# Sample attention: cache pages loaded as 8 KB pieces over every fourth partition, a chunk's loads issued together

## The reference

```python
k_past = cache_k[l][page_table].reshape(bs, past_len, A_HEADS, A_HEAD_DIM)
v_past = cache_v[l][page_table].reshape(bs, past_len, A_HEADS, A_HEAD_DIM)
...
s = jnp.einsum('bqhd,bkhd->bhqk', qi, k, preferred_element_type=jnp.float32) * scale
s = s + fi.transpose(0, 2, 1)[..., :, None] - fk_t[..., None, :]
s = jnp.where(mask, s, -jnp.inf)
p = jax.nn.softmax(s, axis=-1)
return jnp.einsum('bhqk,bkhd->bqhd', p.astype(v.dtype), v)
```

## Time and profile before

| | |
|---|---|
| median of three runs | 3746.3 us (3746.05 to 3747.52) |
| span of the profiled execution | 3747.3 us |
| busy: TensorE, VectorE, ScalarE, GpSimd | 96%, 50%, 48%, 38% of the span |
| sample attention, first value load to last product | about 2,359 to 3,207 us |
| moved by DMA in the span | 590.40 MB, mean 158 GB/s |
| moved in 2,400 to 3,100 us | 232.67 MB, mean 332 GB/s |

### The profile page before, as it was taken

The page is one execution under the profiler, slowest core; times in us unless marked ns, Lnnn a source line. Parts: engine busy times, 40 slices in busy tenths (PEclk is TensorE's granted clock), DMA queues, the critical chain, the costliest instruction groups (busy, mean ns, idle before and its releaser), DMA issues. The chain is left out here.

```text
span 3747.3 us, 54477 instructions
## 1 busy us (share of the span) xinstructions
PE 3585.3 (96%) x17931; PEld 2823.4 (75%) x17931; DVE 1867.7 (50%) x3105; ACT 1810.5 (48%) x3712; POOL 1423.5 (38%) x1072
## 2 busy tenths in 40 slices
PE   8999999999999999999799999899999999799999
PEld 7788888788878888888566666677777777588787
DVE  3134423332123543322557665588888888544432
ACT  4224423445323443543566767677777777311222
POOL 0011122220011122310477777577777777322200
PEclk9999999999999999999799999999999999899999
DMA  4234334324233334333201211699999999544422
GB/s 164 77 120 132 115 128 145 122 96 139 97 108 115 127 132 155 118 126 88 61 18 40 60 38 63 225 329 335 340 335 334 319 338 326 208 155 162 150 90 76
DMA packets 378555, 590.40 MB, mean 158 GB/s; under 512 B 93381, under 2 KB 114485, under 8 KB 378298
## 3 DMA queue, kind: packets, MB, share of 16 engines
q1 hardware_dynamic: 366146, 579.94, 45.9%
q10 hardware_dynamic: 11584, 5.13, 0.5%
q0 software_dynamic: 576, 2.10, 0.2%
HBM read 475.25 MB, written 111.83 MB: 157 GB/s over the span
## 5 line engine op out<-in xcount | busy, mean ns | idle before, releaser
L996 PE MATMUL prj_z_ps<-prj_w_hi,prj_h_hi 128*128 128x512 f32 x2312 | 923.9, 400 | 2.8 <-DVE prj_w_lo L792 2.7
L998 PE MATMUL prj_z_ps<-prj_w_hi,prj_h_lo 128*128 128x512 f32 x2312 | 902.6, 390 | 0.0
L997 PE MATMUL prj_z_ps<-prj_w_lo,prj_h_hi 128*128 128x512 f32 x2312 | 901.2, 390 | 0.0
L1912 POOL TENSOR_TENSOR sa_v_lo<-sa_v_raw,sa_v_hi 128x1024 fp32r<-128x1024 f32 x256 | 609.1, 2402 | 219.7 <-DVE sa_v_hi L2051 219.2
L998 PEld LDWEIGHTS prj_z_ps<-prj_w_hi,prj_h_lo 128*128 128x128 f32 x2312 | 434.3, 188 | 93.7
L996 PEld LDWEIGHTS prj_z_ps<-prj_w_hi,prj_h_hi 128*128 128x128 f32 x2312 | 435.2, 188 | 90.0 <-DVE prj_w_lo L792 5.7
L997 PEld LDWEIGHTS prj_z_ps<-prj_w_lo,prj_h_hi 128*128 128x128 f32 x2312 | 435.3, 188 | 84.8
L1408 POOL TENSOR_TENSOR pa_p_lo<-pa_probs,pa_p_hi 128x512 fp32r<-128x512 f32 (+1 forms) x320 | 367.6, 1164 | 160.9 <-ACT pa_p_hi L1421 143.5
L2045 DVE TENSOR_TENSOR sa_kT_lo<-sa_t_ps,sa_kT_hi 128x512 fp32r<-128x512 f32 x512 | 345.5, 686 | 141.9 <-ACT sa_kT_hi L1934 138.7
L424 POOL TENSOR_TENSOR prj_dist<-prj_cum 128x256 f32<-128x256 f32 x132 | 88.6, 671 | 793.5 <-DVE prj_cum L863 793.5
L1934 ACT CAST sa_kT_hi<-sa_t_ps 128x512 fp32r<-128x512 f32 x512 | 291.1, 590 | 128.6 <-PE sa_t_ps L2198 120.0
(11 more groups left out here) (330 smaller groups left out, 6417.7 us busy)
## 6 DMA issues: line engine op xcount, KB each, us to landing
arena_k_raw<-in_cache_k_dram SPq DMA_DIRECT2D x512, 256.0 KB, 4.1
sa_v_raw<-in_cache_v_dram SPq DMA_DIRECT2D x512, 256.0 KB, 4.3
arena_w_raw<-in_w_main_dram SPq DMA_DIRECT2D x272, 256.0 KB, 4.2
z_scratch<-prj_z_sb SPq DMA_DIRECT2D x272, 256.0 KB
arena_mg<-z_scratch SPq DMA_DIRECT2D x51, 512.0 KB, 4.4
arena_cu<-extp_scratch SPq DMA_DIRECT2D x48, 256.0 KB
arena_x_in<-in_x_all_dram SPq DMA_DIRECT2D x17, 512.0 KB, 3.7
prj_aux<-z_scratch SPq DMA_DIRECT2D x34, 256.0 KB, 2.8
```

The lines of the kernel that those rows point to most:

```text
L996: pe.matmul(out, h_hi[:, slot_of(t), k], hi, start=(k == 0), stop=False)
L997: pe.matmul(out, h_hi[:, slot_of(t), k], lo, start=False, stop=False)
L998: mm = pe.matmul(out, h_lo[:, slot_of(t), k], hi, start=False, stop=(k == KC - 1))
L1912: pool.tensor_tensor(v_lo[:, w % 2, at], v_raw[:, w % RING, at], v_hi[:, w % 2, at].bitcast(F32), ALU.subtract).then_inc(vlo_ready, 1)
```

## The change

A page is still 256 KB and still one DMA. Before, token p of page j went to partition p, 2 KB long, at place j of the slot. Now the page is cut in 32 pieces of four tokens, 8 KB each, and piece r of page j goes to partition 4r + j, filling the whole slot there. Over the four pages of a chunk every partition is filled. At place i of partition 4r + j stands now token 4r + i of page j. Keys and values are laid out alike, so scores and weights agree. The decay rows must follow: ScalarE's `place` reads them in the order place, piece, page instead of straight through.

The waits before the loads are gathered. All four key pages now wait for the four turns of chunk g-3, and all four value pages for both halves of the value chunk three before.

```diff
@@ begin_sample
-                        src = k_view[bass.ds(pages[j], 1)].rearrange("a k x -> (a k) x")
-                        sp.dma_start(arena.k_raw[:, g, j], src).then_inc(arena.k_loaded[g], 16)
+                        src = k_view[bass.ds(pages[j], 1)].rearrange("a (r i) x -> (a r) i x", i=CHUNK_PAGES)
+                        sp.dma_start(arena.k_raw[j::CHUNK_PAGES, g], src).then_inc(arena.k_loaded[g], 16)
@@ attend_sample, sync
             def page(at, j, dst, view, sem):
-                sp.dma_start(dst[:, j], view[bass.ds(at, 1)].rearrange("a k x -> (a k) x")).then_inc(sem, 16)
+                sp.dma_start(dst[j::CP], view[bass.ds(at, 1)].rearrange("a (r i) x -> (a r) i x", i=CP)).then_inc(sem, 16)
 
             def load_k(g, slot, pages):
+                sp.wait_ge(turned, (g - RING + 1) * CP)
                 for j in range(CP):
-                    sp.wait_ge(turned, (g - RING) * CP + (j + 1))
                     page(pages[j], j, k_raw[:, slot], k_view, k_loaded[slot])
 
             def load_v(w, slot, pages, first=False):
+                if not first:
+                    sp.wait_ge(vlo_ready, (w - RING + 1) * 2)
                 for j in range(CP):
-                    if not first and j % (CP // 2) == 0:
-                        sp.wait_ge(vlo_ready, (w - RING) * 2 + (1 if j == 0 else 2))
                     page(pages[j], j, v_raw[:, slot], v_view, v_loaded[slot])
@@ attend_sample, scalar
             def place(g):
                 act.wait_ge(d_loaded[g % 2], 16 * (g // 2 + 1))
                 wait_from(act, added, g - 1)
-                act.copy(addend[0:2 * HEADS, g % 2], d_raw[:, g % 2]).then_inc(d_placed, 1)
+                by_row = d_raw[:, g % 2].rearrange("h (j r i) -> h i r j", j=CP, i=CP)
+                act.copy(addend[0:2 * HEADS, g % 2].rearrange("h (i r j) -> h i r j", i=CP, j=CP), by_row).then_inc(d_placed, 1)
```

## The result

The changed kernel is slower: 3792.89 us median of four runs (3787.2 to 3797.68), against 3746.91 (3746.05 to 3747.78). The ratio on record is 1.0117, 95% interval 1.0104 to 1.0130 (the two medians alone give 1.0123). 3733 us was forecast. The profiled execution took 3787.2 us, with a span of 3785.5, 38.2 us longer than before's.

A forecast was written before the change was run, and what follows sets the result against it. A chain of GpSimd freeing value slots, SyncE's value then key loads, and TensorE was taken to stall chunks. Key waits -14 us, ScalarE +1, made -13 from the 3746.3 median: 3733 us, range 3722 to 3739.

The forecast's parts named there:

- Link 1: SyncE before the value loads: all four value pages wait for GpSimd's second half, fourth key issue 0.76 us later.
- the turn shown: Worked example from the earlier trace: GpSimd done at 2642.84, keys landed by 2651.9, TensorE resumes at 2651.94.
- the far end: Slow end of the forecast: key landing stays at 5.0 us, 0.25 us per chunk lost, +32 us.
- Link 3: Key loads in 8 KB pieces: 405 GB/s instead of 332, last page landing in 3.65 us, keys 0.6 us earlier.
- the break-even of 4.24: Landing time of the last key page, 5.0 - 0.76 us, above which Link 1 outweighs the faster landing.
- The gain: TensorE's key waits, 18.7 us in 109 chunks, 21.4 over the stage; two thirds won, -14 us.
- ScalarE's copy: Strided placing copy: 0 to 0.62 us over 615 ns, covered by the next copy's idle time; 1 us counted.
- link 2: SyncE before the key loads: the batched wait for four turns of chunk g-3 costs nothing, they being long past.
- the start of the stage: First key bursts pause there, values start up to 1.6 us later but are wanted three chunks on: nothing.
- B: Rival: waiting for the whole value slot on SyncE decides, 0 to 0.25 us per chunk, +21, 3767 us; chance 0.18.
- Rival C: Loads get slower, long pieces overlapping worse: 300 GB/s, 7.1 us per chunk, +85, 3831 us; chance 0.05.
- the coarser rule: Only transfers spanning all 128 partitions reach all 16 ports; for 32 partitions half of 332 GB/s, 12.8 us per chunk.

The follow-up runs named there:

- e1_waits: Kernel before with only the key and value waits gathered, 2 KB pieces and plain placing copy kept: 3770.91 us, ratio 1.0057.
- e8_4kb: Pages in 64 pieces of 4 KB over every second partition, values going out by halves, keys waiting pair by pair, placing copy in two: 3782.71 us, ratio 1.0091.
- e3_order_new: Changed kernel with SyncE's order altered, values of chunk g-3 instead of g-2 behind the keys of chunk g: 3746.57 us, ratio 0.9996.
- e4_order_old: Kernel before with SyncE's order altered, values of g-3 behind keys of g, 2 KB pieces and page-wise waits: 3743.98 us, ratio 0.9987.
- e9_slow_waits4: Kernel before with gathered waits and four idle waits ahead of each 2 KB cache load to lengthen SyncE's issue: 3786.35 us, ratio 1.0098.

## Why the prediction was wrong

**Link 1, the gathered value wait: the right mechanism, its size put at less than half.** I had the fourth key issue 0.76 us late in the turn shown. In the turn of the changed kernel it is 1.59 - 0.11 + 0.24 = 1.72 late. The missing 0.96 is the issue step, taken from the earlier trace rows as 0.52 us although the changed load has another shape. It is 0.66: the value burst takes 2.44 us instead of 1.88, the three key steps 1.99 instead of 1.55, together 1.00; reaction and gap make the rest. The gathered wait alone cost +22 us in e1_waits, inside the +32 that I had put as the far end. The far end of the whole change was built from the 0.76 too, 0.25 us per chunk; the key waits grew by 55.4 / 104 - 18.7 / 109 = 0.36 us per chunk, 45 us in all.

**Link 3, the larger pieces: wrong.** In the prediction the sign hung on this step. I took 405 GB/s from weight loads in the earlier trace rows; per full share the changed kernel moves 345, before 342. The last keys of the turn landed 4.3 us after their issue, not 3.65, which is beyond the break-even of 4.24 even for the cheaper issue. With link 1 as it was measured, a landing of 3.65 would not have saved this turn either, since the break-even falls to 5.0 - 1.72 = 3.3: either error alone takes away the gain, both together make the loss.

The traces say what the 405 was made of. By their packet records a piece in 2,400 to 3,100 us took 94.3 ns on the mean at 2 KB in the kernel before, 188.3 at 4 KB in e8_4kb and 373.8 at 8 KB in the changed kernel, which is 21.7, 21.8 and 21.9 bytes per ns. During the merge's weight loads 2 KB and 4 KB pieces ran side by side in the kernel before:

```profile
3224.00:3232.00 8.00, 8.00 (x38) 6.48 (x37) 6.59 (x7) 6.48 (x8) 0.00 (x0) 0.94 1.04 398
```

Here they took 87.0 and 163.7 ns, 23.5 and 25.0 bytes per ns. So more than half of the higher rate came with the place and only the rest with the length, and of the length nothing was left in the sample attention. Why the loads are slower there stays open; idle engines around the weight loads were not it, since TensorE, VectorE and ScalarE are busy in this row.

**SyncE's own cycle was missing.** I counted the step as a delay to the keys and not as an occupation. Two bursts of 2.43 and 2.44 us, the table reads and the gaps are 6.04 us, against 5.92 that TensorE needs; before they were 5.26. This is no bound by itself, since e3_order_new has the same 6.04 and loses nothing. It counts because the key loads stand behind the newest value wait: what SyncE waits there it can no longer make up in the next turns.

**The gain was overpriced.** The wait of 18.7 us was read on the weight-load side, where it runs beside the products before it. With all key waits gone, e4_order_old gained 5 us, nearer to the 6.7 us of the matmul side; part of the gain went to the waits for VectorE, 32.8 us in 110 chunks there where they were 28.1 in 109. When waits are added, the weight-load side was the better guide: in e1_waits 37.1 / 106 - 18.7 / 109 = 0.18 us per chunk, times 125 is 22 us, as measured, and 45 in the changed kernel.

**ScalarE's copy** took 1.15 us, near the upper bound of 1.23, and cost nothing, as said. The key wait (link 2) cost nothing either, as SyncE never waited for a turn; nor did the start of the stage and what follows it.

Of the rivals B came true, with the mechanism and place it names, but at a higher price than its 21 us, since the longer issue adds to it. Rival C, slower loads, did not come true for every fourth partition. The Trainium skill (SBUF — State Buffer, "Door 1: The DMA port swizzle") has it that the ports are chosen by the partition's bits, so that every fourth partition reaches all ports and 32 neighbours only half of them. The runs agree in the direction: 345 GB/s per full share against 234 and 275. The 12.8 us per chunk that the prediction works out for the coarser rule did not come; it was 6.73.

What stays open is whether 8 KB pieces would gain anything at an equal issue cost. With e9_slow_waits4 as the nearest comparison, they don't. Under the altered order they did spare the DMA engines some time, 333 / 0.94 = 354 GB/s per full share against 336 / 0.98 = 343 with 2 KB pieces, but nothing waited for it.

## What to carry to other kernels

A queue that issues loads is an engine with a cycle of its own: add up its issues, table reads and gaps per step of the loop and hold that against the bound of the stage before giving it longer instructions or gathering its waits. Close to the bound it can't make up a wait. In a ring of loads, put the load that is wanted first ahead of the wait that is granted last; that alone brought back all that this change lost. A layout that needs a whole slot free before its first page can go out also takes away the overlap of waiting and issuing, and its issue should be measured in its own shape.

## What the runs showed that was not expected

- The issue of a load whose rows lie two or four partitions apart takes 0.47 to 0.55 us on SyncE, that of neighbouring rows 0.32 to 0.33, whether 32 or 128 of them.
- Pieces of 8 KB instead of 2 KB changed the rate from 342 to 345 GB/s per full share in the stage, though 2 KB and 4 KB pieces ran at 23.5 and 25.0 bytes per ns beside each other in the merge.
- Gathered waits and a turn of 6.04 us on SyncE beside 5.92 on TensorE cost some 45 us while the key loads stood behind the newest value wait, and nothing once that wait was for an older chunk's values.
- A copy on ScalarE of 512 elements with an innermost step of 128 elements takes 1153 ns instead of 615.
